# DeltaNet inverse: full-array block products replaced by 64 by 64 products in two quarters of the array, and the next head's work moved between its six levels

## What is computed

```
lmat = where(strict, einsum("bhnik,bhnjk->bhnij", kb, k) * decay, 0.0)
tinv = triangular_solve(eye + lmat, eye, left_side=True, lower=True, unit_diagonal=True)
u = tinv @ (v * beta[..., None])
w = tinv @ (kb * exp(gc)[..., None])
# then over the chunks: v_new = u - w @ S;  o = qg @ S + attn @ v_new;  S = S * glast + kdec^T @ v_new
```

## Time and profile before

| what | us |
|---|---|
| median of 3 runs (2334.29 to 2340.81) | 2338.1 |
| the profiled execution | 2336.3 |
| its span | 2334.2 |
| PE busy, PEld busy | 2110.1, 1314.7 |
| DVE, ACT, POOL busy | 995.9, 540.4, 276.2 |
| L743 (X products) and L751 (DT products), PE busy | 127.3, 126.9 |
| L760 (turns of D), PE busy | 77.4 |

### The profile page before, as it was taken

The page is one execution under the profiler, slowest core; times in us unless marked ns, Lnnn a source line. Parts: engine busy times, 40 slices in busy tenths (PEclk is TensorE's granted clock), DMA queues, the critical chain, the costliest instruction groups (busy, mean ns, idle before and its releaser), DMA issues. The chain is left out here.

```text
span 2334.2 us, 25709 instructions
## 1 busy us (share of the span) xinstructions
PE 2110.1 (90%) x10098; PEld 1314.7 (56%) x10098; DVE 995.9 (43%) x1920; ACT 540.4 (23%) x1283; POOL 276.2 (12%) x325
## 2 busy tenths in 40 slices
PE   3799999999968999999999998999999794898985
PEld 1555555555545777877777777455555444443432
DVE  4456546465545555555555554000000086222224
ACT  1322323223212434334334344000000000111111
POOL 0020020200210111111021120000000000321102
PEclk9899999999978999999999999999999895899998
DMA  8121111210011101100101010893241544699973
GB/s 300 52 63 46 27 37 46 64 46 23 23 50 29 28 14 41 28 15 28 33 23 28 15 37 8 266 288 108 81 135 28 225 167 198 202 402 412 396 304 140
DMA packets 177799, 259.97 MB, mean 111 GB/s; under 512 B 14759, under 2 KB 146664, under 8 KB 163344
## 3 DMA queue, kind: packets, MB, share of 16 engines
q1 hardware_dynamic: 151096, 219.04, 27.3%
q10 hardware_dynamic: 18488, 23.54, 3.5%
q0 software_dynamic: 8096, 15.75, 1.9%
HBM read 231.78 MB, written 39.10 MB: 116 GB/s over the span
## 5 line engine op out<-in xcount | busy, mean ns | idle before, releaser
L673 PE MATMUL bank<-hT,shared 128*128 128x512 f32 x384 | 180.6, 600 | 8.0 <-DMA shared<-in_w_in_dram 8.0
L1433 PE MATMUL bank<-hT,shared 128*128 128x512 f32 x384 | 169.3, 594 | 2.6 <-DVE xT L1806 1.8
L2405 PE MATMUL bank<-ring,xgT 128*64 128x512 f32 (+1 forms) x416 | 150.6, 632 | 15.4 <-DMA ring<-in_w_exp_up_dram 11.3
L1488 PE MATMUL bank<-wz,hT 128*128 128x512 f32 x320 | 153.0, 616 | 0.0
L1201 DVE TENSOR_TENSOR X<-bank,negm 128x512 f32<-128x512 f32 x144 | 81.8, 598 | 133.9 <-PE bank L743 133.8
L751 PE MATMUL bank<-DT,X 128*128 128x128 f32 x960 | 126.9, 276 | 4.0 <-DVE X L1201 4.0
L743 PE MATMUL bank<-D_,MT 128*128 128x128 f32 x960 | 127.3, 283 | 0.0
L1987 DVE SCALAR_TENSOR_TENSOR prod<-gth,bank 128x512 f32<-128x512 f32 x16 | 11.0, 687 | 272.6 <-PE bank L1957 272.6
L751 PEld LDWEIGHTS bank<-DT,X 128*128 128x128 f32 x960 | 118.1, 192 | 14.8 <-issue 8.4
L743 PEld LDWEIGHTS bank<-D_,MT 128*128 128x128 f32 x960 | 118.7, 198 | 0.9
L1433 PEld LDWEIGHTS bank<-hT,shared 128*128 128x128 f32 x384 | 71.1, 190 | 84.3 <-issue 84.1
(11 more groups left out here) (409 smaller groups left out, 3453.5 us busy)
## 6 DMA issues: line engine op xcount, KB each, us to landing
shared<-in_w_in_dram SPq DMA_DIRECT2D x62, 512.0 KB, 5.7
ring<-in_w_exp_gate_dram SPq DMA_DIRECT2D x26, 1024.0 KB, 11.9
ring<-in_w_exp_up_dram SPq DMA_DIRECT2D x26, 1024.0 KB, 19.4
ring<-in_w_exp_down_dram SPq DMA_DIRECT2D x26, 1024.0 KB, 15.4
aw<-in_w_ada_dram SPq DMA_DIRECT2D x8, 2048.0 KB, 9.9
yd<-mzero ACTq DMA_DIRECT2D x1, 16128.0 KB, 106.8
aw<-in_w_ada_dram SPq DMA_DIRECT2D x8, 1024.0 KB, 21.5
wz<-in_w_in_dram SPq DMA_DIRECT2D x4, 2048.0 KB, 7.8
```

The source lines that it names most:

```text
L673: pe.matmul(bank[LATB[j]][:, :], wof(j)[:, k, :], hT[:, k, SEQ:T], start=(k == 0), stop=(k == KD - 1), skip_group_check=True)
L1433: pe.matmul(bank[a][:, :], wn(n)[:, k, :], hT[:, k, SEQ:T], start=(k == 0), stop=(k == KD - 1))
L1488: last = pe.matmul(bank[Z][:, :], hT[:, k, t * P:(t + 1) * P], wz[:, k, :], start=(k == 0), stop=(k == KD - 1), skip_group_check=True)
L2405: last = pe.matmul(bank[2 + slot][at, :], xgT[:, slot, k, at], wgu[w][:, k, :, :], start=(k == 0), stop=(k == KD - 1))
```

## The change

All in `deltanet`. (1) In levels 0 to 4 a unit's X and DT products are each two products of 64 by 64, on the diagonal quarters of the array, upper left and lower right in turn. (2) In level 5 each is one product of 64 by 64, on the single off-diagonal quarter that is not zero, or the diagonal quarter it comes from; masks, D and DT copies of that level take only those quarters, and the mask is a multiplication by -1. (3) Group 2's DT is put into PSUM by an identity product like the others'. (4) The fills are dealt out anew: Q's steps over levels 1 and 2, V's over 2 to 4 with its context part first (a semaphore of its own, `g_vctx`), the turn of raw k to level 3 and bank 6, the sums of k and q apart (k in level 3, q in the chain after `segments`), the powers on GpSimd apart as well, `mask_att` from level 0 to level 2, V's convolution and silu to the start of its own head's inverse. (5) The prologue has the same new order.

```diff
 def blocks_X(h, l, g):
             for u in range(m):
-                last = pe.matmul(xdv(g)[:, u * P:(u + 1) * P], MT[:, u0 + u, :], D_[:, u0 + u, :], start=True, stop=True, skip_group_check=True)
+                a, b = same(u0 + u), other(u0 + u)
+                if l < LEVELS - 1:
+                    for c in (a, b):
+                        last = pe.matmul(tiles4(xdv(g))[c, u, c], MT[c, u0 + u, c], D_[c, u0 + u, c], start=True, stop=True, skip_group_check=True)
+                else:
+                    last = pe.matmul(tiles4(xdv(g))[b, u, a], MT[a, u0 + u, b], D_[a, u0 + u, a], start=True, stop=True, skip_group_check=True)
...
 def between(h, par, l, i, first, more):
             if l == 1:
-                if more:
+                if more and i < 3:
...
-            if l == 2 and more and i > 0:
+            if l == 2 and more:
+                if i == 0:
+                    proj(n, Q, 3)
                 if i == 1:
                     pe.wait_ge(s["g_v"], h + 1)
-                proj(n, V, i - 1)
-            if l == 3 and more and i == 0:
-                pe.wait_ge(s["g_raw"], 3 * n + 2)
-                proj(n, V, 4)
-            if l == 3 and more and i == 4:
-                turn_k(n)
-            if l == 4 and more and i == 1:
-                sums(n)
+                    proj(n, Q, 4)
+                if i == 3:
+                    pe.wait_ge(gw[V], 16 * n + 16)
+                    proj(n, V, 0)
+            if l == 3 and more:
+                if i == 0:
+                    pe.wait_ge(s["g_raw"], 3 * n + 2)
+                    proj(n, V, 4)
+                if i == 1:
+                    proj(n, V, 1)
+                if i == 3:
+                    turn_k(n)
+                if i == 4:
+                    sums(n, 1)
+            if l == 4 and more:
+                if i == 0 or i == 2:
+                    proj(n, V, 2 + i // 2)
...
 def inverse(h, par, first=False, more=True):   # TensorE
                 pe.wait_ge(s["g_D2"], 3 * h + g + 1)
-                if g < 2:
-                    pe.matmul(dtv(g), C(C_ID), flat(DT[:, u0:u0 + m, :]), start=True, stop=False, skip_group_check=True)
+                pe.matmul(dtv(g), C(C_ID), flat(DT[:, u0:u0 + m, :]), start=True, stop=False, skip_group_check=True)
...
 # VectorE
+            convolve(h, V)
             for l in range(LEVELS):
                 mask_X(h, l)
                 if l == 0:
-                    mask_att(h, par)
+                    silu(h, par, V)
...
-                if more and 2 <= l <= 3:
-                    silu(n, 1 - par, l - 2)
-                if more and 1 <= l <= 2:
-                    convolve(n, l - 1)
+                if more and l == 1:
+                    convolve(n, K)
+                if l == 2:
+                    if more:
+                        silu(n, 1 - par, K)
+                    mask_att(h, par)
                 if more and l == 3:
-                    convolve(n, V, taps=range(2))
+                    convolve(n, Q)
                 if more and l == 4:
-                    keep_sums(n)
-                    convolve(n, V, taps=range(2, TAPS))
+                    keep_sums(n, 1)
+                    silu(n, 1 - par, Q)
                     keep_kn(n, 1 - par)
...
 # TensorE, before head 0
-        for j in (K, Q, V):
+        for j in (K, Q):
...
+        pe.wait_ge(s["g_raw"], 2)
+        proj(0, V, 4)
+        proj(0, V, 0)
+        proj(0, V, 1)
         turn_k(0)
-        sums(0)
+        sums(0, 1)
+        proj(0, V, 2)
+        proj(0, V, 3)
         turn_kn(0, 0)
         for b in range(3):
             products(0, 0, b)
+        sums(0, 0)
```

More of the change, by code:

```diff
@@ L693, in turn_k, with sums @@
                 def turn_k(n):
[L694 removed]
+                    pe.wait_ge(s["g_raw"], 3 * n + 2)
+                    pe.wait_ge(s["g_rawctx"], n + 1)
                     pe.wait_ge(s["g_silu"], 3 * n + 1)
[L696 to L704, removed]
+                    turned(kraw, 6, P, s["g_kturn"])
+                def sums(n, a):
+                    pe.wait_ge(s["g_sq"], 2 * n + 2 - a)
+                    for t in range(NT):
+                        at = 2 * P + a * NT + t
+                        last = pe.matmul(bank[7][:, at:at + 1], sq[:, a, t, :], cst[:, C_ONE, 0:1], start=True, stop=True, skip_group_check=True)
+                    last.then_inc(s["g_sumk" if a else "g_sumq"], 1)
                 def turn_kn(n, par):
                     pe.wait_ge(s["g_kn"], n + 1)
[L708 removed]
+                    turned(kn[:, par, :, :], 6, 3 * P, s["g_knturn"])
                 def turn_v(h, more):
@@ L969, in keep_D @@
                     act.wait_ge(s["g_Dturn"], 18 * h + turn + 1)
-                    act.copy(D_[:, u0:u0 + m, :], tiles4(xdv(g))).then_inc(s["g_Dkept"], 1)
+                    if turn < 3 * (LEVELS - 1):
+                        act.copy(D_[:, u0:u0 + m, :], tiles4(xdv(g))).then_inc(s["g_Dkept"], 1)
+                    else:
+                        for u1, k in kinds(g):
+                            a = same(u1)
+                            last = act.copy(D_[a, u1:u1 + k, a], tiles4(xdv(g))[a, u1 - u0:u1 - u0 + k, a])
+                        last.then_inc(s["g_Dkept"], 1)
                 def keep_DT(h, l, g):
@@ L974, in keep_DT @@
                     act.wait_ge(s["g_DT"], 18 * h + 3 * l + g + 1)
-                    act.copy(DT[:, u0:u0 + m, :], tiles4(dtv(g))).then_inc(s["g_DTkept"], 1)
+                    if l < LEVELS - 1:
+                        act.copy(DT[:, u0:u0 + m, :], tiles4(dtv(g))).then_inc(s["g_DTkept"], 1)
+                    else:
+                        for u1, k in kinds(g):
+                            a, b = same(u1), other(u1)
+                            last = act.copy(DT[a, u1:u1 + k, b], tiles4(dtv(g))[a, u1 - u0:u1 - u0 + k, b])
+                        last.then_inc(s["g_DTkept"], 1)
                 def squares_o(h):
@@ L991, in inverse @@
                             keep_v(h)
-                        if more and 1 <= l <= 2:
-                            raw(n, l - 1)
-                        if more and 2 <= l <= 3:
-                            tanh(n, l - 2, wait=(l == 3 or not first))
+                        if more and l == 1:
+                            raw(n, K)
+                        if more and l == 3:
+                            raw(n, Q)
+                        if more and l == 2:
+                            tanh(n, K)
                         keep_DT(h, l, 0)
+                        keep_DT(h, l, 1)
                         if more and l == 3:
-                            raw(n, V)
-                        keep_DT(h, l, 1)
+                            raw_ctx_v(n)
+                        if more and l == 4:
+                            tanh(n, Q)
                         if l < LEVELS - 1:
@@ L1004, in inverse @@
                         keep_DT(h, l, 2)
+                        if more and l == 5:
+                            square(n, 1 - par, Q)
                         if l < LEVELS - 1:
@@ L1010, in inverse @@
                                 square(n, 1 - par, K)
-                            if more and l == 3:
-                                square(n, 1 - par, Q)
+                            if more and l == 4:
+                                raw(n, V)
                             keep_D(h, 3 * l + 5, 2)
@@ L1129, in begin, with convolve @@
                     TS(out=neg[:, par, :, :], in0=cur[:, par, 1, :, :], scalar1=-1.0, scalar2=None, op0=ALU.mult).then_inc(s["g_cur"], 1)
-                def convolve(n, j, first=False, taps=range(TAPS)):
+                def convolve(n, j, first=False):
                     to, x = conv[:, j % 2, :], padded[:, j % 2, :]
-                    for k in taps:
+                    for k in range(TAPS):
                         if k == 0:
@@ L1199, in mask_X @@
                         dve.wait_ge(s["g_X"], 18 * h + 3 * l + g + 1)
+                        if l == LEVELS - 1:
+                            for u1, k in kinds(g):
+                                a, b = same(u1), other(u1)
+                                last = TS(out=X[b, u1:u1 + k, a], in0=tiles4(xdv(g))[b, u1 - u0:u1 - u0 + k, a], scalar1=-1.0, scalar2=None, op0=ALU.mult)
+                            last.then_inc(s["g_Xkept"], 1)
+                            continue
                         mask = negm[:, l, g:g + 1, :].broadcast_to([P, m, P]) if g < 2 else negm[:, l, :, :]
@@ L1265, in chain @@
                         last.then_inc(s["g_R"], 1)
+                        if more and p == 0:
+                            keep_sums(n, 0)
                         if more and 2 <= p <= 3:
@@ L1292, in chain @@
                             last.then_inc(s["g_osum"], 1)
-                        if more and p == 0:
-                            silu(n, 1 - par, V)
                         if more and p == 1:
```

97 lines of the change are left out of this document (59 added, 38 removed).

## The result

The changed kernel took **2284.2 us** (median of 4 runs, 2281.28 to 2288.24) against 2337.1 for the kernel before in the same session (4 runs). The ratio is 0.977, 95% interval 0.975 to 0.980: 2.3% faster. The forecast was 2281.

A forecast was written before the change was run, and what follows sets the result against it. The prediction took TensorE's instruction stream to bound a steady head; -41 (seven heads), -4.5 (last head) and -11.5 (prologue) made -57, from 2336.3 to 2279, plus 1.8 for the median: 2281 us. Range 2264 to 2325.

The forecast's parts named there:

- A pair of quarters takes one slot: Levels 0 to 4: two 64 by 64 products run together in 0.057 us, a unit costing 0.114 instead of 0.224.
- pairs do not run together: Rival, 13%: the two quarters of a pair are serialised, a unit costs 0.228, and the kernel slows to 2368 us.
- The changes of size: Steady head: 25 stretches of small products, each 0.15 going in and 0.15 or 0.20 coming out, together +8.2 us.
- The inverse: From level 0's first DT product to `products`: six levels adding up to 53.0 us, against 59.4 before.
- The wait before level 5's DT products: TensorE's 1.00 us wait for a late VectorE there goes, as K power and `keep_kn` come earlier.
- the walk misses waits: Rival, 20%: tight slacks lose half a microsecond per level, giving 2301 us, or 2307 with the prologue's gain halved.
- The head: A steady head's period falls by 5.9 us, to 87.3 instead of 93.2; seven such heads give -41.
- the clock falls: Rival, 2%: half-array stretches lower the clock; a quarter of the inverse at 1.2 GHz gives about 2380 us.
- The walk: Level-by-level timing of the new order; before `products`, K's copy ends 1.37 us after the last product, 0.3 more.
- The last head: Without projections to fill it: -1.0 us in each of four levels, -1.5 for ends, +1 for `mask_att`, together -4.5.
- The prologue: Before head 0's inverse: `keep_M` near 725.8, 12.4 us earlier; -11.5 after V's convolution delays the first masks by 0.9.
- The sum: Whole kernel: -41 for seven steady heads, -4.5 for the last one, -11.5 for the prologue, together -57 us.

The follow-up runs named there:

- experiment 1: The changed kernel with the products of levels 0 to 4 on the full array again; 2306.1 us, ratio 0.988 to the kernel before.
- experiment 7: The changed kernel with DT of group 2 in levels 0 to 4 on the full array; 2276.8 us, ratio 0.974.
- experiment 5: The kernel of experiment 4 with each level's DT products in one stretch and X products in another, quarters kept; 2237.3 us, ratio 0.957.
- experiment 6: The kernel of experiment 5 with full-array products in levels 0 to 4; 2292.5 us, ratio 0.980.
- experiment 9: The changed kernel with two useless 256-column products put into the pause before `products`; 2278.3 us, ratio 0.975.
- experiment 3: The changed kernel with all upper left quarters of a group issued first, then all lower right ones; 2323.3 us, ratio 0.994.
- experiment 8: The kernel before with only the prologue's order on ScalarE and VectorE changed; 2331.8 us, ratio 0.997.
- experiment 4: The changed kernel with normalised k turned before level 5's first DT products and its copy first on ScalarE; 2265.9 us, ratio 0.970.

## Why the prediction was right

**A pair of quarters takes one slot: right.** Predicted 0.057, measured 0.058. The rival *pairs do not run together* (13%) did not happen: the two quarters' records start 7 ns apart. The Trainium skill (TensorEngine Tiling, Restrictions and Gotchas) says that different row tiles cannot access the same PSUM bank at the same time; this trace does not agree for two quarters on the diagonal, with results in different partitions of one bank.

**The changes of size: right,** and the decisive step. Predicted 8.2 a head for 25 stretches, measured 0.345 x 25 = 8.6 by experiment 1; experiments 7, 5 and 6 put a stretch at 0.32, 0.34 and 0.30. Experiment 7 shows that the price belongs to the change, not to the product, and experiment 5 that it can be had back by merging.

**The inverse: right.** Predicted levels 10.6, 10.7, 10.1, 10.0, 8.2 and 3.4; measured 10.9, 10.8, 10.1, 10.1, 8.2 and 3.2. Together 53.2 against 53.0. The wait before level 5's DT products is gone, as said. The rival *the walk misses waits* did not happen: level 0 is 0.3 longer than the sum, the others are within 0.2 of it.

**The head: half a step missed.** Predicted 87.3, measured 87.1 in a head at full clock, but 88.8 in four heads and some of it in a fifth. The rival *the clock falls* looked for it in the half-array products. In heads 0 to 6 the inverse stays at 1.00 in the changed kernel; the clock falls behind the pause that follows it. The walk had seen that K's copy is late, and had priced it as lateness (0.3); it is late by 0.2 (1.12 for 0.89), and the price is what `products` and the records behind it then take longer: 1.68 in each of four heads and 1.27 in the fifth (against experiment 9), 8.0 together. The last head is 1.1 longer in experiment 9 (36.9 against 35.7), at a granted clock of 0.91 against 0.95: the fall that comes with its wait of 2.74 lasts longer there. The medians are 5.9 apart. Nothing in the trace of before says that 0.89 is harmless and 1.12 is not: experiment 3 has the same pause and never a slow `products`, experiments 1 and 7 have it in three heads and in one. What else decides it is open.

A stop is not the only thing that stands before a fall. In the kernel before, the clock falls in heads 0, 3 and 6 with TensorE busy throughout, behind the sums of level 4, 20 records with one moving column each. Head 3, the sums and what follows (four turns take 0.60 elsewhere), then the granted clock of the stretch from those turns on, 0.50:

```profile
1075.36 2.29 PE L703 MATMUL bank<-cst,gboth 128*128 128x1 f32 x20
...
1078.52 1.06 PE L760 MATMUL bank<-cst,DT 128*128 128x128 f32 x4
```

```profile
1078.52:1081.08 2.56, 2.56 (x13) 2.56 (x13) 2.49 (x6) 1.20 (x3) 1.95 (x1) 0.50 0.00 0
```

It costs 0.32 in head 3 (93.48 against 93.16). The prediction had read the clock of head 4 and of the prologue, and took the prologue for the place where it falls; these falls it had not seen. Experiment 3, which has no fall at `products`, has one of this kind in head 0, behind 10 such records and 16 of quarters: four records of a projection take 3.66 instead of 1.98, and the head 93.7 instead of 92.0.

```profile
787.41 1.28 PE L711 MATMUL bank<-cst,gboth 128*128 128x1 f32 x10
...
789.51 3.66 PE L678 MATMUL bank<-hT,shared 128*128 128x512 f32 x4
```

So the rival's idea, that thin work lets the clock fall, is not refuted by the changed kernel; what holds is that its own inverse, heads 0 to 6, shows no such fall.

**The last head: low.** Predicted -4.5, measured -6.1. No experiment took it apart.

**The prologue: right in size.** Predicted `keep_M` at 725.8, 12.4 earlier; measured 728.21 with the first projection 3.04 later, so 13.1 earlier relative to it. Predicted -11.5 to the first DT product, measured -12.5. Rows of the changed kernel, VectorE, GpSimd, TensorE:

```profile
719.77 0.16 DVE L1220 TENSOR_SCALAR ssum<-bank 128x5 f32<-128x5 f32 x1 [3.84 <-PE bank L711]
...
728.21 1.94 DVE L1247 TENSOR_TENSOR MT<-bank,D_ 128x256 f32<-128x256 f32 x6
```

```profile
720.01 1.20 POOL L1129 TENSOR_TENSOR rn<-ssum,half 128x5 f32<-128x5 f32 x1 [26.35 <-DVE ssum L1220]
```

```profile
738.24 0.68 PE L767 MATMUL bank<-DT,X 64*64 64x64 f32 x16 [0.88 <-DVE X L1270]
```

The power of 5 elements took 1.20 and not the 1.58 assumed, `products` ended at 727.09, which is 0.25 ahead of the forecast 724.3 when the 3.04 are taken off, and the wait for X was 0.88, as said of V's convolution (0.9). The forecast took TensorE at full clock here, with the remark that some of the gain goes if it is cold; it was not cold at `products` (2.43 for ten records, experiment 8).

The sum was -57 and the span's difference -54.3. Heads 0 to 6 gave 34.3 instead of 41 (+6.7: the clock took 8.0, and the heads without it gave 1.3 more than the sum), the prologue -1.6, the last head -1.6, and stages that the change does not touch -0.8 (chance, no part of the forecast). The large terms were right; the misses are small and partly cancel.

## What to carry to other kernels

Price a small tile by its stretches, not by its products: here a 64 by 64 pair saves 0.108 a unit and each stretch of it costs 0.30 to 0.345, so a stretch pays from three or four units on, and merging stretches (experiment 5 on 4) gave 29 us more, above the 22 that the quarters gave in the order before. A stop of about a microsecond on the bound engine can cost more behind it than in it: look at the granted clock of the run that follows each wait, and put work into the stop, by moving it there or even by adding it. Test a change that has two parts by each part alone; here the pairs of levels 0 to 4 alone gave 22 of 53 us, and the rest of the change alone 31.

## What was not expected of the hardware

- TensorE starts products for another quarter of the array ahead of earlier ones for a busy quarter, about 5 slots of 0.058 (experiment 3). It hides the order of issue for 4 slots a quarter, and two fifths of what 8 slots a quarter would lose; over the kernel the serial order still cost 39 us against pairs.
- 1.12 us without work, and the next 3.2 us ran at a granted clock of 0.55, in 5 of 7 heads (head 6 shows it in 2.90 between the first and the eighth start of `products`, instead of 1.62); in experiment 9, with 0.9 us of the stop filled, in none. Experiment 3 has the stop of 1.12 in all heads and no fall behind it. The kernel before has falls to 0.50 without any stop, behind 20 records of one column.
- Two records of different quarters start 7 ns apart and write one PSUM bank.
